# A transformer layer: the gate projections by seven block products instead of eight, and who does the convolution's sums and the low parts

## The reference

```
proj = x @ w_in + b_in                         # 1024 x 4608
glu_in, q, k, v, gate_logits = split(proj, [1024, 1536, 2048, 2560])
u = a * sigmoid(gate), a and gate the halves of glu_in
u = depthwise causal conv, 31 taps, 512 channels; u = silu(layer_norm(u, over channels))
y_conv = u @ w_conv_out
y_attn = chunked_attention(q, k, v, rel_bias) @ w_attn_out      # 8 heads of 64
g_conv, g_attn = split(sigmoid(gate_logits))                    # 1024 x 1024 each
mixed = (g_conv * y_conv + g_attn * y_attn) @ w_o + b_o
x = layer_norm(alpha * x + mixed)
x = layer_norm(alpha * x + grouped top-2 mixture of 16 experts(x))
```

## Time and profile before

| | us |
|---|---|
| median of 3 executions | 1135.71 |
| lowest and highest | 1132.48, 1136.20 |
| span of the profiled execution, first to last instruction | 1130.7 |
| TensorE busy | 1098.3 |
| VectorE busy | 803.2 |
| ScalarE busy | 529.2 |
| GpSimd busy | 227.4 |

### The profile page before, as it was taken

The page is one execution under the profiler, slowest core; times in us unless marked ns, Lnnn a source line. Parts: engine busy times, 40 slices in busy tenths (PEclk is TensorE's granted clock), DMA queues, the critical chain, the costliest instruction groups (busy, mean ns, idle before and its releaser), DMA issues.

```text
span 1130.7 us, 17012 instructions
## 1 busy us (share of the span) xinstructions
PE 1098.3 (97%) x5583; PEld 913.1 (81%) x5584; DVE 803.2 (71%) x1152; ACT 529.2 (47%) x787; POOL 227.4 (20%) x190
## 2 busy tenths in 40 slices
PE   8999999999999999999999999999999999999984
PEld 7888888888978789878888888787888888888762
DVE  5799999935447766666685588888679556558866
ACT  5111111123456665645331134467578545557755
POOL 0000000000046864757100000013121211212110
PEclk9999999999999999999999999999999999999998
DMA  7121233232111010181632325889999876699966
GB/s 266 56 84 56 83 104 104 83 112 93 57 38 43 19 43 1 65 326 39 251 118 88 142 119 196 278 331 354 324 331 381 311 230 192 236 352 341 368 177 269
DMA packets 49800, 199.58 MB, mean 177 GB/s; under 512 B 7249, under 2 KB 7633, under 8 KB 47682
## 3 DMA queue, kind: packets, MB, share of 16 engines
q1 hardware_dynamic: 43538, 176.19, 41.9%
q0 software_dynamic: 6192, 22.49, 8.0%
HBM read 166.21 MB, written 32.52 MB: 176 GB/s over the span
## 4 chain that ended last, share of the span: by engine, by line
PE 85%; DVE 4%; DMA 4%; ACT 3%; POOL 2%; issue 2%; ACTq 0%; DVEq 0%; SPq 0%; POOLq 0%
PE ps L544 16%; PE ps L546 16%; PE ps L545 16%; PE ps L1570 9%; PE ps L1572 9%; PE ps L1571 9%; PE ps L644 2%; PE ps L630 2%; DMA gu<-in_wexp 2%; PE ps L616 2%; DMA dn_raw<-in_wexp 2%; PE ps L1651 1%; PE ps L1566 1%; POOL pr L499 1%; PE ps L1678 1%
## 5 line engine op out<-in xcount | busy, mean ns | idle before, releaser
L544 PE MATMUL ps<-xh,wh 128*128 128x512 f32 x512 | 203.3, 397 | 2.0 <-DVE xl L1030 1.7
L545 PE MATMUL ps<-xl,wh 128*128 128x512 f32 x512 | 199.5, 390 | 0.0
L546 PE MATMUL ps<-xh,wl 128*128 128x512 f32 x512 | 199.5, 390 | 0.0
L1469 DVE TENSOR_TENSOR gu<-gu (+1 forms) x128 | 148.6, 1220 | 33.6 <-issue 21.5
L499 POOL TENSOR_SCALAR pr<-pr,rinv 128x640 f32<-128x640 f32 (+4 forms) x64 | 95.4, 1503 | 379.7 <-DVE rinv L1153 379.5
L1052 DVE SCALAR_TENSOR_TENSOR cv<-u,dw_t,cv 128x1024 f32<-128x1024 f32 x120 | 154.1, 1284 | 3.7
L1570 PE MATMUL ps<-gu,xgh 128*128 x336 | 134.0, 399 | 4.0 <-DVE gu L1469 2.2
L1463 ACT ACTIVATE gu<-gu (+1 forms) x128 | 124.4, 1048 | 20.6 <-DMA gu<-in_wexp 13.0
L1572 PE MATMUL ps<-gu,xgl 128*128 x336 | 131.9, 393 | 0.0
L1571 PE MATMUL ps<-gu,xgh 128*128 x336 | 131.4, 391 | 0.0
L544 PEld LDWEIGHTS ps<-xh,wh 128*128 128x128 f32 x512 | 96.1, 188 | 25.4 <-issue 6.4
(11 more groups left out here) (278 smaller groups left out, 2022.4 us busy)
## 6 DMA issues: line engine op xcount, KB each, us to landing
gu<-in_wexp SPq DMA_DIRECT2D x64, 1024.0 KB, 9.1
dn_raw<-in_wexp SPq DMA_DIRECT2D x16, 2048.0 KB, 9.8
raw<-in_wblk SPq DMA_DIRECT2D x52, 512.0 KB, 4.2
gate_cols<-gst SPq DMA_DIRECT2D x16, 512.0 KB, 5.3
xf<-acc_rows SPq DMA_DIRECT2D x8, 512.5 KB, 8.1
xraw<-in_xT SPq DMA_DIRECT2D x8, 512.0 KB, 7.3
gcm<-gate_cols SPq DMA_DIRECT2D x8, 512.0 KB, 7.5
gam<-gate_cols SPq DMA_DIRECT2D x8, 512.0 KB, 14.5
```

The costliest lines, as they stand in the source:

```text
L544: pe.matmul(o, a_h, b_h, start=first, stop=False)
L545: pe.matmul(o, a_h, b_l, start=False, stop=False)
L546: return pe.matmul(o, a_l, b_h, start=False, stop=last)
L1469: eng.tensor_tensor(gu[:, par, k, 1, :], gu[:, par, k, 1, :].bitcast(F32), gu[:, par, k, 0, :], ALU.subtract).then_inc(gu_lo, 1)
```

## The change

The gates of one 128-column pair q (column block q of g_conv and column block q of g_attn) are written as a 2 x 2 block product: weights split by branch n and by halves of the 1024 input channels, x by halves of channels and halves of tokens. Instead of eight products of halves (512 channels deep, 512 tokens wide) seven are computed, on sums of weight quarters and sums of x quarters (Strassen's scheme in Winograd's form), and 7 additions on their results give the four outputs. So the gate stage is 8 pairs x 7 products (`UNITS`, 56), 12 matmuls each.

- The four sums of x quarters are made on VectorE before the first GLU product (`input_sums`), each split in high (ScalarE) and low part (VectorE).
- The four sums of weight quarters per pair are made in memory: GpSimd copies a quarter by DMA from memory to memory and adds others onto it by accumulating DMAs (`weight_sums`), in seven rounds, each waiting until the round before has landed.
- Weights of products come as units of 256 KB through eight slots; their low parts are GpSimd's, as are those of blocks 3 to 13.
- The results' additions are VectorE's (`gate_sums`), between one or two taps for each product; the sigmoids follow on ScalarE in 512-column pieces, and the stores are 256 KB each.
- The convolution's running sum lies in psum banks 6 and 7 and only the last tap of a channel block writes `cv`. Eight taps stand behind each GLU block. The GLU blocks take banks 0 to 5 in turn.
- Mean and variance come after the gates: `conv_mean` before the first value tile, `conv_var` before tile 5; centring, reciprocal (in four pieces) and normalising lie beside the value tiles and behind them. The matmul is with ones, the factor 1/512 is applied when its result is read.
- Scaling the bias of the first two head pairs goes from VectorE to GpSimd.
- Some semaphores are shared and some tiles moved by half a KB.

```diff
-TAPS_A_STEP = 7
+TAPS_A_STEP = 8
+VAR_TILE = 5
...
+UNIT_SLOTS = 8
+PARTS = {1: (0, 0), 2: (0, 1), 4: (1, 1)}
+SUMS = {5: 0, 6: 1, 7: 2, 3: 3}
+ORDER = (1, 6, 5, 7, 2, 3, 4)
+T_ROWS = {5: 0, 7: 1, 6: 2, 4: 3}
+UNITS = [(x, q) for q in range(KC) for x in ORDER]
+N_UNITS = len(UNITS)
+GATES_STORED = 16 * KC // 2
...
+        def gate_weights(q, n, k):
+            return wblk[W_GATE + 2 * q + n][:, CB * k:CB * k + CB, :]
+        def sum_round(x, q):
+            return q // 2 + {5: 1, 7: 1, 6: 2, 3: 3}[x]
+        def sums_issued(r):
+            return sum(2 * many for g in range(KC // 2) for stage, many in enumerate((4, 2, 1, 1)) if g + stage <= r)
+        U2, W, U3, C22, C11, C12, C21 = range(1, 8)
...
+        def glu_bank(n):
+            return 2 * (n % 3)
+        def unit_bank(m):
+            return (m + 4) % 6
...
+                def weight_sums(g, stage):
+                    if not 0 <= g < KC // 2:
+                        return
+                    for q in (2 * g, 2 * g + 1):
+                        s1, s2, s3, s4 = (wsum_dram[i, q] for i in range(4))
+                        of = (((s1, gate_weights(q, 1, 0)), (s3, gate_weights(q, 0, 0)), (s2, gate_weights(q, 0, 0)), (s4, gate_weights(q, 0, 1))),
+                              ((s1, gate_weights(q, 1, 1)), (s3, gate_weights(q, 1, 0))), ((s2, s1),), ((s4, s2),))[stage]
+                        for o, a in of:
+                            if stage:
+                                pool.dma_start(o, a, accum_op=ALU.add, max_dma_last_dim=4096).then_inc(wsum_in, 16)
+                            else:
+                                pool.dma_start(o, a).then_inc(wsum_in, 16)
+                def sums_round(r):
+                    if r:
+                        pool.wait_ge(wsum_in, 16 * sums_issued(r - 1))
+                    for stage in range(4):
+                        weight_sums(r - stage, stage)
+                def unit_low(m):
+                    s = m % UNIT_SLOTS
+                    pool.wait_ge(u_hi, m + 1)
+                    pool.tensor_tensor(ul[:, s], uraw[:, s], uh[:, s], ALU.subtract).then_inc(u_lo, 1)
+                pool.wait_ge(x_hi, KC)
+                pool.wait_ge(w_lo, 3)
+                for n in range(B_V[0] - 3):
+                    low(n + 3)
+                    for r in (2 * n, 2 * n + 1):
+                        if r < KC // 2 + 3:
+                            sums_round(r)
+                for m in range(N_UNITS):
+                    unit_low(m)
+                for n in range(B_V[0], B_Q[0] + 2):
+                    low(n)
+                scale_bias(0)
+                scale_bias(1)
+                for n in range(B_Q[1], B_Q[1] + 2):
+                    low(n)
...
+                def gate_product(m):
+                    x, q = UNITS[m]
+                    s, bank = m % UNIT_SLOTS, unit_bank(m)
+                    pe.wait_ge(u_lo, m + 1)
+                    if m < 2:
+                        pe.wait_ge(sig_ready, CB - 1)
+                    elif m < 4:
                         pe.wait_ge(u_ready, CB)
+                    elif m < 6:
+                        pe.wait_ge(sig_ready, CB)
                     else:
-                        pe.wait_ge(g_sig, {14: 12, 15: 14}.get(g, g - 3))
-                    weights_left(B_GATE + g, 2 * (gate_q(g) % 4))
+                        bank_read(m - 6)
+                    if x in T_ROWS:
+                        pe.wait_ge(x_lo, KC + T_ROWS[x] + 1)
+                        b_h, b_l = t_high[T_ROWS[x]], t_low[T_ROWS[x]]
+                    else:
+                        b_h, b_l = (quarter(a, *{1: (0, 0), 2: (1, 0), 3: (1, 1)}[x]) for a in (xh, xl))
+                    for k in range(CB):
+                        last = mm3(ps[:, bank, :], uh[:, s, k], ul[:, s, k], b_h[:, k, :], b_l[:, k, :],
+                                   k == 0, k == CB - 1)
+                    last.then_inc(blk_used, 1)
...
+                    for n in (2 * j, 2 * j + 1):
+                        if n >= 3:
+                            pe.wait_ge(sig_ready if n % 2 == 0 else u_ready, (n - 3) // 2 + 1)
+                        weights_left(n, glu_bank(n))
+                for m in range(N_UNITS):
+                    gate_product(m)
                 conv_mean()
-                gate_job(LAST_GATES[0])
-                conv_var()
-                gate_job(LAST_GATES[1])
                 pe.wait_ge(w_lo, B_V[0] + 2)
                 for t in range(TT):
-                    if t < 2:
-                        pe.wait_ge(cent, CB)
-                    elif t < 4:
-                        pe.wait_ge(g_sig, N_GATE - 1)
+                    if t < 4:
+                        bank_read(N_UNITS - 6 + t)
                     else:
                         pe.wait_ge(v_lo, t - 3)
-                    v_tile(0, t, ps[:, 4 + t % 4, 0:2 * P])
+                    if t == VAR_TILE:
+                        conv_var()
+                    v_tile(0, t, ps[:, V_BANKS[t % 4], 0:2 * P])
                 for i in range(2):
                     pe.wait_ge(w_lo, B_Q[0] + i + 1)
-                    if i:
-                        pe.wait_ge(g_sig, N_GATE)
-                    else:
-                        pe.wait_ge(std_done, 1)
+                    pe.wait_ge(v_lo, TT)
...
+                    so_far = psf[:, 6 * HALF:8 * HALF]
                     if k == 0:
-                        dve.tensor_scalar(cv[:, j, :], tap, w, cpar[:, 0, j:j + 1], ALU.mult, ALU.add).then_inc(conv_d, 1)
+                        if i:
+                            dve.wait_ge(conv_d, i)
+                        dve.tensor_scalar(so_far, tap, w, cpar[:, 0, j:j + 1], ALU.mult, ALU.add).then_inc(conv_d, 1)
                     else:
                         dve.wait_ge(conv_d, i)
-                        dve.scalar_tensor_tensor(out=cv[:, j, :], in0=tap, scalar=w, in1=cv[:, j, :],
+                        dve.scalar_tensor_tensor(out=so_far if k < CW - 1 else cv[:, j, :], in0=tap, scalar=w, in1=so_far,
                                                  op0=ALU.mult, op1=ALU.add).then_inc(conv_d, 1)
...
+                def input_sums():
+                    dve.tensor_tensor(t_raw[0], quarter(xraw, 0, 0), quarter(xraw, 0, 1), ALU.subtract).then_inc(t_sum, 1)
+                    dve.wait_ge(zero_out, 32)
+                    dve.tensor_tensor(t_raw[1], quarter(xraw, 1, 1), quarter(xraw, 0, 1), ALU.subtract).then_inc(t_sum, 1)
+                    dve.wait_ge(t_sum, 2)
+                    dve.scalar_tensor_tensor(out=t_raw[2], in0=t_raw[0], scalar=-1.0, in1=quarter(xraw, 1, 1),
+                                             op0=ALU.mult, op1=ALU.subtract).then_inc(t_sum, 1)
+                    dve.wait_ge(t_sum, 3)
+                    dve.scalar_tensor_tensor(out=t_raw[3], in0=t_raw[2], scalar=-1.0, in1=quarter(xraw, 1, 0),
+                                             op0=ALU.mult, op1=ALU.subtract).then_inc(t_sum, 1)
+                def gate_sums(m):
+                    x, q = UNITS[m]
+                    slot = lambda i: gst[:, q % 2, i, :]
+                    def add(which, o, a, b, after=None, stored=None):
+                        if after is not None:
+                            dve.wait_ge(c_sum, sum_no(after, q))
+                        if stored is not None and q >= 2:
+                            dve.wait_ge(row_moved[4 * (q % 2) + stored], 16 * (q // 2))
+                        assert sums_made[0] + 1 == sum_no(which, q)
+                        sums_made[0] += 1
+                        dve.tensor_tensor(slot(o), a, slot(b), ALU.add).then_inc(c_sum, 1)
+                    if x == 1:
+                        return
+                    dve.wait_ge(blk_used, B_V[0] + m + 1)
+                    o = ps[:, unit_bank(m), :]
+                    if x == 6:
+                        dve.wait_ge(c_copy, q + 1)
+                        add(U2, 1, o, 0, stored=1)
+                    elif x == 5:
+                        add(W, 2, o, 1, U2, 2)
+                    elif x == 7:
+                        add(U3, 1, o, 1, W)
+                        add(C22, 3, ps[:, unit_bank(m - 1), :], 1, U3, 3)
+                    elif x == 2:
+                        add(C11, 0, o, 0)
+                    elif x == 3:
+                        add(C12, 2, o, 2)
+                    else:
+                        add(C21, 1, o, 1)
+                sums_made = [0]
...
+                def some_taps(n):
+                    nonlocal taps
+                    for i in range(taps, min(taps + n, CB * CW)):
+                        conv_tap(i)
+                        taps = i + 1
+                        if taps % CW == 0 and taps > CW:
+                            column_sum(i // CW)
+                input_sums()
+                for i in range(4):
+                    dve.wait_ge(x_hi, KC + i + 1)
+                    dve.tensor_tensor(t_low[i], t_raw[i], t_high[i], ALU.subtract).then_inc(x_lo, 1)
+                for n in range(2, B_V[0]):
```

(54 more changed lines are left out.)

326 lines of the change are left out of this document (183 added, 143 removed).

## The result

| | before | after |
|---|---|---|
| median of the runs, us | 1134.6 (1132.48 to 1136.2, 4 runs, the three above among them) | 1164.43 (1162.02 to 1167.64, 4 runs) |
| span of the profiled execution, us | 1130.7 | 1160.2 |
| TensorE's mean granted clock | 0.991 | 0.971 |

The ratio is 1.0263, 95% interval 1.0236 to 1.0290: slower, where 1130.9 us was forecast. The time lies beyond the upper end of the range (1119 to 1156), on the side of rival C.

A forecast was written before the change was run, and what follows sets the result against it. The number of TensorE matmuls (97% busy) was taken as the bound. The terms -21.7 + 15.8 + 1.1 = -4.8 us gave span 1125.9, time 1130.9 us with 5.0 carried over; range 1119 to 1156.

The forecast's parts named there:

- rival C: In the GLU blocks accumulating data set the pace at 1.85 us each; blocks 39.7 us late, 1154.8 us; chance 0.30.
- Term 3: GLU blocks: low parts queued behind 64 DMAs on GpSimd, whose issues set the pace; TensorE loses 15.8 us.
- The issue at 0.85 us: GpSimd's weight-sum rounds: issuing one direct DMA holds GpSimd for 0.85 us, ends 0.43 and 1.6.
- The data "under 0.85": Weight-sum rounds: moving 256 KB, accumulating or not, takes under 0.85 us, ends 0.65 and 1.85.
- The tail "2.0 for the last 256 KB": Weight-sum rounds: the last 256 KB lands 2.0 us after a round's last issue.
- Term 1: Gates on TensorE: 672 matmuls instead of 768, 96 removed at 0.2263 us each, 21.7 us less.
- Term 2: VectorE ahead of the gates: input sums and taps delay the last GLU product before product 2; 6.8 us lost.
- Rival D: VectorE's taps: a tap through psum is dearer, say 1.55 us; +10 us, 1141 us; chance 0.10.
- term 4: Behind the gates: mean and variance work hidden beside value tiles; queries wait 1.1 us for the last value tile's low part.
- The 5.0 us between span and time: Whole kernel: median of the runs lies 5.0 us above the profiled span, carried over from before to after.
- A: The forecast itself: GpSimd's DMA issue at 0.85 us sets the pace, 1130.9 us, own range 1124.8 to 1137.2; chance 0.38.

The follow-up runs named there:

- e2: The changed kernel with its 32 accumulating DMAs made plain copies of the same 256 KB, weight sums left out; 1157.92 us, one execution.
- e6: e1 with low 3 on VectorE, GpSimd's next lows behind VectorE's x-sum low parts, first GLU product between those, seven taps; 1120.25 us, ratio 0.9868.
- e1: The changed kernel with another order on GpSimd alone: same DMAs, late rounds behind unit low parts; 1128.56 us, ratio 0.9960.
- e3: The changed kernel without the 64 weight-sum DMAs and their waits, products loading plain weight quarters; 1128.19 us, one execution.
- e4: e1 with the convolution's running sum in SBUF (cv) instead of psum; 1172.98 us, ratio 1.0326.

## Why the prediction was wrong

**Term 3 failed**, "issues set the pace": it was put at 15.8 us and measured 48.6. That is 32.8 of the 34.3 us by which the span missed (1160.2, forecast 1125.9). It rested on three choices.

- The issue at 0.85 us: measured 0.52 for a copy and about 0.53 by pitch for an accumulating DMA. This one was too dear.
- The data "under 0.85": e2's copies held the engines for 0.81 us each, and an accumulating DMA comes to 1.60 (the estimate above). So accumulating DMAs and not issues set the pace. This is the step that failed. By e2 it is worth 22.6 us of wait.
- The tail "2.0 for the last 256 KB": GpSimd idled 6.7 to 10.4 us after a round's last issue, 5.8 to 8.3 behind the copies of e2.

With copies that cost no more than the prediction said, TensorE still waited 21.0 us where the sum had 15.8: the longer tail, less what the cheaper issues gave back, is the other 5. Low 5 came at 96.2 (forecast 74.6), low 6 at 120.2 (89.2), low 7 at 131.9 (93.3). The estimate that the prediction sets beside its sum by the Trainium skill, "DMA: Bandwidth & Descriptors", section "Anatomy of one DMA", is 0.6 us of data for 256 KB and a fixed part of 2.0; the measurements are above both, for copies too, and they decide.

The failure was one of choice. The only row of an accumulating DMA said 1.85 us for 256 KB; I set it aside for an odd row length and took a value from issue costs, another resource. The tail came from a transfer out of SBUF, and the 405 GB/s that stood for the other end from the experts' stage, whose weights are loaded into SBUF; these DMAs read memory and write memory.

**Rival C was right in the main and too small.** It forecast low 5 at 82.8 and low 6 at 113.1, blocks 39.7 us late, 1154.8 us. Measured were 48.6, of which low 6 at 120.2 is 7.1 and a restart at 1.2 GHz on block 6 1.7 (the one on block 5 lies inside the wait for low 6). Of the 7.1, 4.1 are there before round 1 is issued (36.2 us, by the forecast's rounds 32.1): low 3 took 4.24 us beside VectorE, not 2.40, and round 0 landed later. The rest is in rounds 1 to 4. It had waits of some 20 us before blocks 5 and 6; they were 32.2 and 11.4, because low 5 stood behind round 3's pause as well.

**Term 1 was right**: 672 matmuls in 152.2 us, forecast 152.1. The saving stands in every kernel here; e6 is what it looks like with the waits gone.

**Term 2 was right and hidden**, as the prediction had it, with one thing left out. The first GLU product at 40.7 (forecast 39.2), a tap in psum at 1.32 us pitch (15 in 19.84 us, forecast 1.315), and in e1 and e3 the last GLU product 4.8 to 5.6 us late before product 2 (forecast 6.8). Rival D falls: 1.286 us by the row. (With the 3 us that its own sum takes off, it would decide from 1.47 a tap and not 1.44.) The term left out that the 2048-wide sums and low parts read two inputs from SBUF beside GpSimd. In the changed kernel that cost 1.3 us (`t_raw`, 3.56 against 2.28), in e1 and e3 it was a wait of 5.5 to 5.7 us.

**The gates and term 4 were right**: no wait in the gates; the queries wait 1.0 us for the last value tile's low part (forecast 1.1).

**The restarts were missing.** No term had TensorE's clock fall in a wait, though the forecast itself had waits of 12.1 and 3.7 us before blocks 5 and 6. They cost 3.4 us in the changed kernel, 5.5 in e1 and 3.7 in e3.

**The 5.0 us between span and time.** The sum sets the median of three executions against the span of one. In every run on record here the time is 1.7 to 2.5 us above its own span, so some 3 of the 5.0 are scatter between executions. Span against span the miss is 34.3 us, time against time 33.5.

**The chances.** A had 0.38 and C 0.30. Given that the only row for the disputed operation was C's, C should have been the forecast, with 1154.8, and the range drawn around it to beyond 1164.

## What to carry to other kernels

A round of DMAs that waits for the round before costs its data and its landing, not its issue: here 11 to 26 us for a round of 8 to 16 DMAs from memory to memory, of which issuing was 4 to 8 (a pause apart). Put such rounds behind the work that the same queue owes to the bottleneck, or let nothing urgent stand behind them: the same DMAs in another order took the kernel from +2.6% to -0.4%, and with the two element-wise engines kept apart and one tap fewer behind each block to -1.3%. When the trace holds a single row of the disputed operation, forecast from it, and ask of every borrowed rate between which memories it was measured.

## What the runs showed of the hardware

- 64 DMAs of 256 KB from memory to memory, half of them accumulating, moved at 217 GB/s of busy engine time, 64 plain copies at 322 (16.78 MB in 52.1 us). A copy held the engines for 0.81 us, an accumulating one for 1.60 (estimate from the two). With the landing in it a round took 1.1 to 1.4 us for each DMA where all are copies and 1.4 to 1.9 where a third or more accumulate; 6 to 10 us passed from the last issue to the landing of all.
- GpSimd issued direct DMAs of 256 KB at 0.52 us each. With accumulating ones among them it stopped for 9.3 us in round 3 with no semaphore to show for it; with half the space for descriptors it stopped earlier and oftener (4.85, 3.52, 8.07 us), with copies alone not at all. What fills the space, and when it comes free, is not shown.
- VectorE with two inputs in SBUF beside GpSimd's subtractions: 8.85 us for what takes 4.49, and GpSimd 8.04 for 4.8; with the running sum in psum a tap keeps its 1.286 us, in SBUF it takes 1.785 on average. The form without an input in psum pays for writing there: the first tap of a channel block takes 1.34 us into psum and 0.81 into SBUF (before and e4).
- TensorE restarted at the 1.2 GHz level after waits of 32.2 and 11.4 us, and in e1 of 5.7 and 4.8: the first matmuls 0.43 us apart. 1.7 us were lost after the wait of 32.2, 3.1 after that of 4.8.
- In a kernel that routes by value, leaving out part of the computation changes the work behind it: 84 matmuls, 19.0 us. Count them before comparing spans.
